# A two-layer diffusion step on one core: 32 instead of 24 blocks of 128 experts multiplied densely in the last step, with new places for rows, bands and gates

## The reference

```python
q = (xt @ lp["peer_wq"]).reshape(n_tok, PEER_HEADS, 2, PEER_HALF)
s = jnp.einsum("thmd,mhnd->thmn", q, lp["peer_keys"])
v1, i1 = lax.top_k(s[:, :, 0], PEER_TOPK)
v2, i2 = lax.top_k(s[:, :, 1], PEER_TOPK)
...
idx = jnp.take_along_axis(cand_i, pos, axis=-1)   # i1 * 128 + i2
g = jax.nn.softmax(top_s, axis=-1)
act = jnp.einsum("td,thkd->thk", xb, u_tab[ib])
return jnp.einsum("thk,thkd->td", jax.nn.gelu(act) * gb, v_tab[ib])
```

## Time and profile before

| what | us |
|---|---|
| median of 3 runs | 2503.35 (2500.39 to 2504.37) |
| the profiled execution | 2499.15 |
| its span, first to last instruction | 2497.0 |
| POOL issues the last row of step 2 | 1876.60 |
| duo 0 of step 3 is weighed | 1899.94 |
| first and last gate batch on PE | 2032.7 to 2278.5 |
| first and last sum on PE | 2283.7 to 2445.4 |

### The profile page before, as it was taken

How to read it: one execution, slowest core, us unless ns; L and a number is a source line. 1 busy time by engine, 2 the same in 40 slices (tenths; PEclk the granted TensorE clock), 3 DMA queues, 4 the chain that set the end, 5 groups by cost and what they waited for, 6 DMA issues and landing times.

```text
span 2497.0 us, 24844 instructions
## 1 busy us (share of the span) xinstructions
PE 1817.0 (73%) x7834; PEld 840.7 (34%) x7834; DVE 1628.9 (65%) x4613; ACT 358.8 (14%) x1003; POOL 999.7 (40%) x1028
## 2 busy tenths in 40 slices
PE   6899656778447576676646796677985978778995
PEld 2455432354112221123311264235641533333221
DVE  0348984574785456564588689456666669887557
ACT  1321132101010122210001113211111000000000
POOL 0004536544533233333333555644453445444343
PEclk9899788978678787888977898787997989989998
DMA  9989999979889999999999999987997999999997
GB/s 382 406 349 357 385 397 328 351 307 368 299 355 422 423 415 421 421 416 422 422 390 421 383 403 374 352 333 283 351 345 285 383 377 396 374 365 376 391 395 281
DMA packets 167076, 930.31 MB, mean 373 GB/s; under 512 B 26311, under 2 KB 28871, under 8 KB 97007
## 3 DMA queue, kind: packets, MB, share of 16 engines
q0 software_dynamic: 147456, 740.81, 75.5%
q1 hardware_dynamic: 19490, 187.93, 18.4%
HBM read 990.08 MB, written 3.15 MB: 398 GB/s over the span
## 4 chain that ended last, share of the span: by engine, by line
DMA 31%; PE 29%; DVE 18%; issue 14%; another core or an unknown queue 4%; ACT 3%; POOL 1%; SPq 0%; POOLq 0%; DVEq 0%; ACTq 0%
DMA ring<-peer_uv_in,vidx 14%; DMA work<-peer_uv_in,vidx 11%; PE psum L1193 7%; PE acc L1287 5%; PE acc L1309 3%; PE psum L917 3%; DMA wring<-peer_uv_in,vidx 2%; DVE work L2229 2%; DVE ring L2281 2%; DVE work L1733 1%; PE psum L944 1%; PE psum L1243 1%; DVE work L1728 1%; PE acc L843 1%
## 5 line engine op out<-in xcount | busy, mean ns | idle before, releaser
L825 POOL DMA_INDIRECT ring<-peer_uv_in,vidx x428 | 419.2, 979 | 598.8 <-PE acc L1287 194.8
L1287 PE MATMUL acc<-ring,cond 128*32 128x512 f32 x984 | 294.0, 709 | 225.0 <-DVE cond L2193 222.7
L825 POOL DMA_INDIRECT ring<-peer_uv_in,idx x193 | 182.8, 947 | 379.5 <-DVE idx L1865 201.9
L825 POOL DMA_INDIRECT work<-peer_uv_in,vidx x207 | 205.4, 992 | 285.2 <-PE acc L1287 99.2
L2229 DVE CUSTOM_DVE_ANT_0 work<-work,h_kept 128x1024 f32<-128x1024 f32 (+1 forms) x183 | 221.2, 1218 | 98.3 <-DMA work<-peer_uv_in,vidx 92.3
L1287 PE MATMUL acc<-work,cond 128*32 128x512 f32 x732 | 213.3, 695 | 67.3 <-DVE cond L2193 66.3
L2281 DVE CUSTOM_DVE_ANT_0 ring<-ring,h_kept 128x1024 f32<-128x1024 f32 x193 | 224.1, 1216 | 8.5 <-DMA ring<-peer_uv_in,idx 4.1
L2229 DVE CUSTOM_DVE_ANT_0 ring<-ring,h_kept 128x1024 f32<-128x1024 f32 x128 | 153.9, 1218 | 75.5 <-DMA ring<-peer_uv_in,vidx 59.2
L1193 PE MATMUL psum<-work,wring 128*128 128x256 f32 (+1 forms) x896 | 172.8, 353 | 29.2 <-issue 26.2
L1287 PEld LDWEIGHTS acc<-ring,cond 128*32 128x32 f32 x984 | 53.0, 122 | 414.2 <-DVE cond L2193 262.6
L1630 ACT ACTIVATE dots<-dots 128x2 f32<-128x2 f32 x256 | 51.9, 203 | 917.4 <-DVE dots L2229 911.6
(11 more groups left out here) (280 smaller groups left out, 2674.5 us busy)
## 6 DMA issues: line engine op xcount, KB each, us to landing
wring<-w_in_in SPq DMA_DIRECT2D x17, 2048.0 KB
wring<-peer_wq_in SPq DMA_DIRECT2D x14, 2048.0 KB
wring<-mod_w_in SPq DMA_DIRECT2D x10, 2048.0 KB
ring<-mod_w_in SPq DMA_DIRECT2D x9, 2048.0 KB, 11.8
wring<-w_out_in SPq DMA_DIRECT2D x8, 2048.0 KB
wring<-peer_us_in SPq DMA_DIRECT2D x6, 2048.0 KB
wring<-peer_vs_in SPq DMA_DIRECT2D x12, 1024.0 KB, 9.3
work<-mod_w_in SPq DMA_DIRECT2D x5, 2048.0 KB, 14.1
```

Of the source, the lines that this page charges most:

```text
L825: nc.gpsimd.indirect_dma_start(row(kind, k, t, r)[0], None, io["peer_both" if kind == "f" else "peer_one"], bass.IndirectOffsetOnAxis(ap=a ...
L1287: ins = mm(acc[half][lane:lane + QUAD, :], vw_duo(k, t, i)[:, j * QUAD:(j + 1) * QUAD], held[:, D + half * CHUNK:D + (half + 1) * CHUNK], ...
```

## The change

`SHARED` goes from 24 to 32: 4096 experts dense, eight more blocks in the place where scores of tile 1 stood (`expert_acts` now fills columns 2048 to 10240 of `work`). Two more chunks of `peer_us` and four more parts of `peer_vs` are loaded. The remaining 21 blocks of activations stand among the duos, one in 1.45; the gates begin at duo 34, one batch in 1.55; the sums at duo 86, one in 0.5. The slots change: columns 10240 to 14336 of `work` are two slots from row 5 on, instead of three slots from row 11 on; `lent_line` is a slot from row 5. `wring[1]` becomes two slots at row 72 instead of 52. What is cleared shrinks to 1512 columns and moves ahead. The shares `s6` and `s7` come earlier in the choosing, and the third row's dot product goes behind the first product of PE. The pooling bands of the latent steps keep only their 136 columns that aren't zero. In step 0 the chunk 0 of `wq` is loaded behind the keys, and the final norm weights are loaded once.

```diff
@@ -33,0 +34,2 @@
+REACH = 128 + max(POOL_WINDOWS) // 2
@@ -77 +79 @@
-SHARED = 24
+SHARED = 32
@@ -117 +119 @@
-ACTS_FROM, GATES_FROM, SUMS_FROM = 2, 24, 85
+ACTS_FROM, GATES_FROM, SUMS_FROM = 2, 34, 86
@@ -119,2 +121,3 @@
-ACTS_EVERY, GATES_EVERY, SUMS_EVERY = 1.6, 1.85, 0.68
-ACTS_UNTIL, GATES_UNTIL = 52, 174
+INDEXED_ROW = 5
+ACTS_EVERY, GATES_EVERY, SUMS_EVERY = 1.45, 1.55, 0.5
+ACTS_UNTIL, GATES_UNTIL = 72, 176
@@ -169 +172,2 @@
-    lat = np.concatenate(bands[:4], 1).astype(np.float32)
+    lat = np.concatenate([band[:, ti * 2 * P:(ti + 1) * 2 * P][:, ti * (2 * P - REACH):][:, :REACH]
+                          for band in bands[:4] for ti in range(2)], 1).astype(np.float32)
@@ -278 +282 @@
-            L.band = region(10776, 2048)
+            L.band = region(10776, 8 * REACH)
@@ -311 +315 @@
-                L.worn = [region(8 * D, 2 * D), region(12 * D, 2 * D)]
+                L.worn = [region(12824, 14 * D - 12824)]
@@ -314 +318 @@
-                L.gated = [region(15360 + j * BATCH * SHARED, BATCH * SHARED) for j in range(2)]
+                L.gated = [region(17408 + j * BATCH * SHARED, BATCH * SHARED) for j in range(2)]
@@ -554,3 +558,2 @@
-        spare_line(region(10 * D, 2 * D), 2, after_step[STEPS - 1], len(stream))
-        for worn in steps[STEPS - 1].L.worn:
-            spare_line(worn, 2, after_step[STEPS - 1], len(stream))
+        indexed_used = row_no["f", STEPS - 1, 0, INDEXED_ROW]
+        spare_line(region(10 * D, 4 * D), 4, indexed_used, len(stream))
@@ -576 +579 @@
-        line_from = {k: row_no["f", k, 0, LENT_ROW] for k in (1, 3)}
+        line_from = {1: row_no["f", 1, 0, LENT_ROW], 3: row_no["f", 3, 0, INDEXED_ROW]}
@@ -730 +732,0 @@
-                    load_chunk("wq", k, 0)
@@ -741,2 +743 @@
-                    if k or cc:
-                        load_chunk("wq", k, cc)
+                    load_chunk("wq", k, cc)
@@ -753,3 +754 @@
-                if st.lat:
-                    sp.wait_ge(*after("h2", st.k, st.T - 1))
-                else:
+                if not st.lat:
@@ -758,2 +757,2 @@
-                final_w = mod_a if st.lat else hn[st.X]
-                load(final_w[:, :], io["final_norm_w"].rearrange("(a n) -> a n", a=1).broadcast_to([P, D]), "fw_in", st.k)
+                    final_w = io["final_norm_w"].rearrange("(a n) -> a n", a=1).broadcast_to([P, D])
+                    load(hn[st.X][:, :], final_w, "fw_in")
@@ -804,2 +803,3 @@
-                if n == after_step[STEPS - 1]:
-                    pool.wait_ge(*after("cleaned"))
+                if n == indexed_used:
+                    pool.wait_ge(*after("both_indexed", STEPS - 1, 1))
+                    pool.wait_ge(*after("cleaned", 0))
@@ -1029,3 +1029,11 @@
-                        for ti in range(T):
-                            ins = mm(p[64 * r:64 * r + 64, 0:N], st.L.pz[ti][:, g * 64:(g + 1) * 64],
-                                     st.L.band[:, (g * T + ti) * N:(g * T + ti + 1) * N], start=(ti == 0), stop=(ti == T - 1))
+                        to = p[64 * r:64 * r + 64, :]
+                        held = [st.L.pz[ti][:, g * 64:(g + 1) * 64] for ti in range(T)]
+                        if T == 1:
+                            ins = mm(to[:, 0:N], held[0], st.L.band[:, g * N:(g + 1) * N], start=True, stop=True)
+                            continue
+                        near, far = (st.L.band[:, (g * T + ti) * REACH:(g * T + ti + 1) * REACH] for ti in range(T))
+                        both = 2 * REACH - N
+                        mm(to[:, 0:REACH], held[0], near, start=True, stop=False)
+                        mm(to[:, N - REACH:REACH], held[1], far[:, 0:both], start=False, stop=True)
+                        ins = mm(to[:, REACH:N], held[1], far[:, both:], start=True, stop=True)
@@ -1613,0 +1622,5 @@
+                if kind == "c":
+                    act.wait_ge(*after("picked", k, i))
+                    worn = steps[k].L.worn[i]
+                    A(worn, worn, ACT.Copy, scale=0.0).then_inc(*mark("cleaned", i))
@@ -1619,6 +1631,0 @@
-                    if t == 0:
-                        act.wait_ge(*after("picked", k, 1))
-                        for j, worn in enumerate(steps[k].L.worn):
-                            ins = A(worn, worn, ACT.Copy, scale=0.0)
-                        ins.then_inc(*mark("cleaned"))
@@ -2205,2 +2212,2 @@
-                dve.wait_ge(*after("fw_in", st.k))
-                V.scalar_tensor_tensor(x[n][:, :], x[n][:, :], rstd[:, 3:4], (mod_a if st.lat else hn[st.X])[:, :],
+                dve.wait_ge(*after("fw_in"))
+                V.scalar_tensor_tensor(x[n][:, :], x[n][:, :], rstd[:, 3:4], hn[2][:, :],
@@ -2401,0 +2409,3 @@
+BESIDE_DENSE = {("choose", 0, 7): "v23 s6", ("choose", 1, 0): "v24 v25 s7", ("choose", 1, 2): "v28 v29"}
@@ -2404 +2414 @@
-    texts = BESIDE_LATENT | BESIDE_EARLY if early else BESIDE_LATENT | BESIDE_OPENING | {"dt": "u11"}
+    texts = BESIDE_LATENT | BESIDE_EARLY if early else BESIDE_LATENT | BESIDE_OPENING | {"dt": "u11"} | BESIDE_DENSE
@@ -2497,0 +2508,4 @@
+            if steps[k].dense:
+                plan["choose", 1, 0] = plan["choose", 1, 0] + [("c", k, 0, 0)]
+                third = left.pop(left.index(("f", k, 0, 2)))
+                left.insert(left.index(("p", k, 0, 0)) + 1, third)
```

## The result

The changed kernel takes **2548.59 us** (median of 4 runs, 2532.94 to 2557.39), the kernel before in the same session 2503.86 (4 runs). The ratio is **1.0155**, 95% interval 1.0122 to 1.0189: slower, by 39 us (0.0155 x 2503.86), with 30 to 47 in the interval; the two medians are 44.7 apart. Forecast were 2530.4 us, with a range of 2496 to 2552. The profiled execution took 2551.41 us, with a span of 2549.4 against 2497.0 before.

A forecast was written before the change was run, and what follows sets the result against it. DMA was taken to bound the opening, DVE the gates and PE the sums. Last sum at 2479.6 plus tail 45.6 minus 1.2 gave a 2524.0 us span; its 27.0 excess over before, added to 2503.35, gave 2530.4, range 2496 to 2552.

The forecast's parts named there:

- Until step 3: Up to the opening of step 3: early slots let rows 5 to 7 out sooner, row 8 issued at 1901.8 us.
- To duo 34, by DMA: Row 8 to row 69: 61 rows, four chunks of u and final weights at DMA's pace, 143.1 us, until 2044.9.
- the last sentence of the sum: Engine totals: PE gains 8 activation blocks and 16 sums; DMA has 25.9 us less for rows, 19.9 more for weights.
- rival 3: Too few slots until row 72: eight pairs give 2.56 us a row, total 2543.4; sign: row 69 after 2055; chance 0.13.
- Latency and stall to duo 34: From issue of row 69 to weighing duo 34: 12.9 us latency plus 10 for the `count` wait, ends 5 and 12.
- Gates, duos 34 to 86, by DVE: Dense gates in step 3: DVE's work 208.3 us plus 23 idle, ends 12 and 32, makes 231.3 us.
- Sums, by PE: From duo 86 to the last sum: 64 sums, 31 duos and two spreads of h on PE, 180.5 us, ending 2479.6.
- Rival 2: Sums stay with DMA, 161.5 us, PE fitting added sums into its waits for rows: total 2517.4; chance 0.10.
- Tail: From the last sum to the end: 51.6 us before, 6 taken off, ends 0 and 10, leaving 45.6.
- Bands: Narrower pooling bands in steps 1 and 3 save 0.49 MB of loading, 1.2 us, ends 0 and 2.3.
- Rival 1: Only DMA matters throughout step 3, gates 209.4 and sums 161.5 us: faster, total 2485.5; chance 0.15.
- The terms at nothing: Before step 3: keys moved ahead of a `wq` chunk, 0 (gain up to 3); earlier shares, 0 (gain up to 5).

The follow-up runs named there:

- experiment 8: Changed kernel with only the first 4 of 8 terms of each activation product on PE for blocks 11 to 31: 2526.41 us, ratio 1.0096.
- experiment 2: Changed kernel with picks skipped only where the first key is below 24, so 15 MB more rows are fetched: 2553.65 us, ratio 1.021.
- experiment 4: Changed kernel without the second keys' one-hot matrix on DVE for 30 of the 32 batches: 2528.84 us, ratio 1.009.
- experiment 5: Changed kernel with 4 instead of 8 gate products per batch on PE: 2516.14 us, ratio 1.0058.
- experiment 7: Changed kernel with DVE's product of activations and gates one duo later, all work the same: 2523.27 us, ratio 1.0086.
- experiment 1: Changed kernel with SHARED back to 24 and the earlier rates, leaving the slots, places, bands and orders: 2506.17 us, ratio 1.0007 to the kernel before.

## Why the prediction was right, and where it was off

The sign, and the limits of gates and sums as no longer DMA's, came out as forecast: slower, with a chance of 0.81. The median is 18.2 us above the forecast of 2530.4. (The forecast's own range of 2514 to 2550 doesn't follow from its ends, which add up to 2505.4 to 2547.4.) Span against forecast span, 2549.4 against 2524.0, by steps:

1. **Until step 3: +5.9.** Row 8 was issued at 1907.7, forecast 1901.8. Duo 0 was weighed between 1890.0 and 1909.4 in the thirteen profiled kernels with the change's places, and at 1904.6 in the changed kernel, so this is mostly scatter of an execution and not a cost of the change.
2. **"To duo 34, by DMA": +8.3, and the limit named was wrong.** Row 8 to row 69 took 151.4 us (to 2059.15) instead of 143.1. The step priced rows and chunks of `u` and left out what the last sentence of the sum had counted: eight more blocks of activations on PE, 3.7 us each (78.6 us of records for 21 blocks in the opening, against 48.4 for 13 before). With half of these products duo 33 came 12.9 us sooner (experiment 8); with 15 MB more rows, no later (experiment 2). By my own sign, a row 69 later than 2055, rival 3 would have been taken for shown, though its fixed pace wasn't the cause. That the step missed by only 8 us is luck: a price for DMA happened to lie near what PE's work took.
3. **Latency and stall to duo 34: +1.4.** 24.3 us against 12.9 + 10. The wait for `count` was 7.8, in the bounds of 5 to 12.
4. **"Gates, duos 34 to 86, by DVE": +14.0.** The busy part was right: 209.5 us against 208.3. The idle part was 36 us, not 23, and above my end of 32. I had taken DVE's waits of before as they were. But each wait for the gate products, 20.9 us of them against 4.6 before, stops the next duo's weights as well. It isn't "by DVE" then, but by DVE and PE in turn: 22 us go with relief on either, and 18.3 when the product stands a duo later (experiments 4, 5 and 7). So DVE was busy for 0.85 of the stage, not over 0.9.
5. **"Sums, by PE": -1.6, right.** From duo 86 to the last sum 178.9 us against 180.5, and with half the work 161.7 between first and last sum, close to the 161.5 that I had worked out for DMA. Rival 2 would have had 161.5, and so would the rule to judge PE by its weight loads (the Trainium skill, Perfetto Trace Analysis, section Identifying the Most-Contended Engine; the section names beside them the share of peak arithmetic, which I didn't work out). The trace doesn't bear that out: weight loads were busy for 63.2 of the 207.1 us of the last stage, 31%, and PE was the limit all the same. The distance between starts told it.
6. **Tail: -3.9.** 41.7 us against 45.6, in its bounds of 41.6 to 51.6.
7. **Bands: +1.2** in this sum, since the whole reached step 3 later and their gain can't be seen apart.

Before rounding these make +25.4. Rival 1, only DMA, is refuted by the time and by the stages of experiment 2. The terms at nothing (`wq`, keys, shares) were not tried apart; all together, in experiment 1, they show no effect.

## What to carry to other kernels

When DMA is nearly full and work is moved from it to other engines, price that work in every stage that the new limit can reach; I had done it for two of three. A batch that goes DVE, PE, DVE needs a place in the order at which its return is surely there: the same work was 18 us shorter with the last part one duo later, and this must be looked at again whenever the batches move closer. Halving one engine's work at a time shows who is the limit. Where halving either brought the same here, the order between them was the cause, and moving one part, with all the work kept, showed it.
